# Projection chunks spread over the transform stages of a fused Hyena and pooling layer

## What is computed

```python
u = h * (1.0 + scale[:, None, :]) + shift[:, None, :]
proj = u @ w_in[layer] + b_in[layer]
hy_streams, hy_gate, pool_in, pool_gate = jnp.split(proj, splits, axis=-1)
k_freq = _hyena_filters_freq(...)
y_h = _hyena_branch(hy_streams, conv_w[layer], conv_b[layer], k_freq, hyena_bias[layer])
y_p = _pool_branch(pool_in, pool_w[layer], pool_scale[layer])
y = jnp.concatenate([y_h * silu(hy_gate), y_p * silu(pool_gate)], axis=-1)
out = gate[:, None, :] * (y @ w_out[layer] + b_out[layer])
h = _layer_norm(DEEPNORM_ALPHA * h + out, ln_g[layer], ln_b[layer])
```

## Time and profile before

| | us |
|---|---|
| median of 3 runs | 1505.89 |
| lowest, highest | 1505.31, 1510.5 |
| the profiled execution, its own time | 1512.34 |
| its span | 1510.6 |
| TensorE busy in the span | 1226.2 |
| VectorE, ScalarE, GpSimd busy | 837.5, 461.6, 427.1 |

### The profile page before, as it was taken

The page is one execution under the profiler, slowest core; times in us unless marked ns, Lnnn a source line. Parts: engine busy times, 40 slices in busy tenths (PEclk is TensorE's granted clock), DMA queues, the critical chain, the costliest instruction groups (busy, mean ns, idle before and its releaser), DMA issues. The chain is left out here.

```text
span 1510.6 us, 14907 instructions
## 1 busy us (share of the span) xinstructions
PE 1226.2 (81%) x5260; PEld 943.8 (62%) x5260; DVE 837.5 (55%) x784; ACT 461.6 (31%) x619; POOL 427.1 (28%) x236
## 2 busy tenths in 40 slices
PE   3788956489999999999999953784757855699996
PEld 1356734378888888888888732553545534488884
...
GB/s 316 76 258 318 308 348 407 325 134 56 56 112 79 87 168 36 62 83 56 8 49 56 28 249 341 235 275 191 353 333 248 338 207 325 205 168 85 105 89 69
DMA packets 170488, 273.50 MB, mean 181 GB/s; under 512 B 24007, under 2 KB 70087, under 8 KB 167626
## 3 DMA queue, kind: packets, MB, share of 16 engines
...
## 5 line engine op out<-in xcount | busy, mean ns | idle before, releaser
L136 PE MATMUL prj_pp<-u_uhi,prj_whi 128*128 128x512 f32 x768 | 300.2, 391 | 0.2 <-POOL u_ulo L800 0.2
L138 PE MATMUL prj_pp<-u_uhi,prj_wlo 128*128 128x512 f32 x768 | 299.0, 389 | 0.0
L137 PE MATMUL prj_pp<-u_ulo,prj_whi 128*128 128x512 f32 x768 | 299.0, 389 | 0.0
L136 PEld LDWEIGHTS prj_pp<-u_uhi,prj_whi 128*128 128x128 f32 x768 | 144.2, 188 | 30.6 <-issue 0.6
L138 PEld LDWEIGHTS prj_pp<-u_uhi,prj_wlo 128*128 128x128 f32 x768 | 144.2, 188 | 30.4
L137 PEld LDWEIGHTS prj_pp<-u_ulo,prj_whi 128*128 128x128 f32 x768 | 144.2, 188 | 29.5
L808 POOL CAST prj_whi<-prj_ws 128x1024 fp32r<-128x1024 f32 x22 | 23.9, 1086 | 392.5 <-DMA prj_ws<-in_w_in 230.3
L899 ACT ACTIVATE prj_row<-prj_pp,prj_bcol 128x512 f32<-128x512 f32 x64 | 43.9, 688 | 291.1 <-PE prj_pp L138 253.7
L1001 DVE TENSOR_SCALAR prj_cv<-prj_row,prj_cw,prj_cb 128x2048 f32<-128x2048 f32 x12 | 16.2, 1347 | 191.6 <-PE prj_px L844 103.9
L1284 POOL TENSOR_TENSOR sp_y<-sp_by_re,sp_by_im 128x512 f32<-128x512 f32 x32 | 68.2, 2132 | 191.1 <-DVE sp_by_im L1355 191.1
L136 PE MATMUL sp_u<-sp_ahi,spec_fwd 128*128 128x512 f32 x128 | 57.2, 447 | 62.3 <-DVE sp_alo L1335 62.3
(11 more groups left out here) (186 smaller groups left out, 2476.6 us busy)
## 6 DMA issues: line engine op xcount, KB each, us to landing
kseq<-fs_xo SPq DMA_DIRECT2D x32, 512.0 KB, 4.1
fs_a<-kseq SPq DMA_DIRECT2D x32, 512.0 KB, 8.6
kfreq<-fs_out SPq DMA_DIRECT2D x32, 512.0 KB, 9.2
sp_a<-xseq SPq DMA_DIRECT2D x32, 512.0 KB, 5.9
...
bseq<-sp_out SPq DMA_DIRECT2D x32, 512.0 KB, 3.5
prj_ws<-in_w_in SPq DMA_DIRECT2D x24, 512.0 KB, 6.4
...
```

The lines of the kernel that those rows point to most:

```text
L136: nc.tensor.matmul(out, w[0], m[0], start=start, stop=False, skip_group_check=True)
L137: nc.tensor.matmul(out, w[0], m[1], start=False, stop=False, skip_group_check=True)
L138: return nc.tensor.matmul(out, w[1], m[0], start=False, stop=stop, skip_group_check=True)
```

## The change

The projection is no longer a stage. `uhi` and `ulo` (both 64 KB in each partition) are made once and stay in SBUF from the second filter stage to the end of the pooling, and the 96 chunks are written into the other stages: 16 in `values_and_filters` (the old `filter_stage2` with the making of u and the tiles of v), 8 in `signal_stage1`, 16 in the first `spectrum_product`, 8 in `between_orders`, 16 in the second `spectrum_product`, and 32 in a stage `pooling` of their own, with the pooling sums. The class `Projection` holds the resident data, two PSUM banks `pp` and one buffer `ws` for raw weights; `Turned` and `Gated` hold the work that follows a chunk. The stages are named p1 to p6 in the tiles.

The rings are shorter: in `spectrum_product` one buffer each for `ahi`, `alo`, `u`, `y`, `by_im`, `yhi`, `ylo`, `b`, `out` and two for `a` and `kf`; in `between_orders` one `xhi`, one `xlo` and two of the rest, before four.

Also: x and `w_in` come already transposed or tiled as inputs (`t_xt`, `t_win`), so the 128 transposes of x go away; the filter's first step works on pairs of 64-row matmuls without GpSimd's copy `hs`; the forward first step of the signal too (6 half matmuls for 6 whole ones, a table of half the size); the table copies `w1f`, `kgen` to `i1` are made in `front`, those of `w1s` and `iw1` in p1; and the loads of `ya` (4 MB) and `gate_bias` move from sp1 into `last_inverse`.

The core of the diff:

```diff
+    def half_chunk(self, pe, q, half):
+        n, c, b, bank = q // 4, q % 4, q // 4 % 2, q % 2
+        if half == 0:
+            if c == 0:
+                pe.wait_ge(self.wlo_done[b], n // 2 + 1)
+            after(pe, self.bank_read[bank], q // 2)
+        cols = slice(c * CH, (c + 1) * CH)
+        for k in range(4 * half, 4 * half + 4):
+            mm = mm3(self.nc, self.pp[bank][:, :], (self.whi[b][:, k, :], self.wlo[b][:, k, :]),
+                     (self.uhi[:, k, cols], self.ulo[:, k, cols]), k == 0, k == KT - 1)
+        if half == 1:
+            mm.then_inc(self.prj_done[bank], 1)
...
+def values_and_filters(nc, t, tabs, pj, scale1, shift, kseq, kfreq, vx):
...
+        chunk_at = {2 + 2 * q if q < 4 else 9 + 3 * (q - 4) // 2: q for q in range(16)}
+        form_at = {step: (2 * step, 2 * step + 1) for step in range(8)}
+        conv_at = {step + 2: q // 4 for step, q in chunk_at.items() if q % 4 == 3}
+        turn_at = {step + 1 + part: (i, part) for step, i in conv_at.items() for part in range(4)}
...
+            for step in range(S):
+                if 0 <= step - 1 < N:
+                    unit(step - 1)
+                q = due(chunk_at, step)
+                if q is not None:
...
+                    pj.chunk(pe, q)
+                if due(turn_at, step) is not None:
+                    tn.turn(pe, *turn_at[step])
```

In `spectrum_product` (TensorE, VectorE; `conv_at` is every fourth step from 5):

```diff
-            staggered(NU, (fwd, 0), (inv, 3))
+            for step in range(S):
+                if step < NU:
+                    fwd(step)
+                if step < 16:
+                    pj.chunk(pe, q0 + step)
+                if 0 <= step - 1 < NU:
+                    inv(step - 1)
+                if tn and step in turn_at:
...
+                            tn.turn(pe, i, part)
...
-            staggered(NU, (alow, 0), (ylow, 3), (multiply, 1), (real_to_y, 1))
+            for step in range(S):
+                if step < NU:
+                    alow(step)
...
+                if tn and step in conv_at:
+                    tn.conv(dve, conv_at[step])
...
+                if 0 <= step - 1 < NU:
+                    ylow(step - 1)
+                if step < NU:
+                    multiply(step)
```

In `between_orders` (TensorE; SyncE's loads):

```diff
-            staggered(GS, (inv, 0), (fwd, 4))
+            for step in range(S):
+                if step < GS:
+                    inv(step)
+                c = due(chunk_at, step)
+                if c is not None:
+                    pj.half_chunk(pe, q0 + c, 0)
+                if 0 <= step - 3 < GS:
+                    fwd(step - 3)
+                if c is not None:
+                    pj.half_chunk(pe, q0 + c, 1)
...
+                    after(sp, xlo_done, n - 1)
+                    sp.dma_start(x[r][:, :, :], group_rows(bseq, n)).then_inc(x_in[r], 16)
+                    after(sp, inv_done[r], n // 2)
+                    sp.dma_start(f32(itab[r][:, :, :, :]), tabs["iw1"][n, :, :, :, :]).then_inc(itab_in[r], 16)
+                    after(sp, z_done[r], n // 2)
+                    sp.dma_start(x1[r][:, :], vx[:, n, DH:2 * DH]).then_inc(x1_in[r], 16)
```

More of the change, by code:

```diff
@@ L507, in gen @@
             def gen(n):
[L508 to L516 removed]
+                r, g, o = n % 2, n // 2, n % 2
@@ new lines, in _ @@
+            for step in range(S):
+                if step in form_at:
+                    for m in form_at[step]:
+                        form_u(m)
+                if step < N:
+                    low(step)
+                if 0 <= step - 2 < N:
+                    evac(step - 2)
+                if due(conv_at, step) is not None:
+                    if conv_at[step] == 0:
+                        for b in range(4):
+                            dve.wait_ge(ulo_done[b], 4)
+                    tn.conv(dve, conv_at[step])
+                if step in form_at:
+                    low_u(form_at[step][0])
@@ L646, in evac @@
             def evac(n):
[L647 to L670 removed]
+                dve.wait_ge(mm_done[n % 2], n // 2 + 1)
@@ new lines, in evac @@
+                after(dve, stored[n % 3], 16 * (n // 3))
+                nc.vector.tensor_copy(xo[n % 3][:, 1, :], ps[n % 2][:, 1, :]).then_inc(out1[n % 2], 1)
+            for step in range(S):
+                if step < GS:
+                    low(step)
+                if 0 <= step - 2 < GS:
+                    evac(step - 2)
+                c = due(chunk_at, step - 2)
+                if c is not None and c == 3:
+                    gt.conv(dve, 0)
+                if c is not None and c >= 4:
+                    gt.gate(dve, 0, c - 4)
@@ L1495, in last_inverse @@
[L1495 removed]
+def last_inverse(nc, t, tabs, bseq, rows, g2, ya, gate_bias, whl):
     with Scope(nc, "fin") as s:
```

1744 lines of the change are left out of this document (918 added, 826 removed).

## The result

The changed kernel takes 1446.23 us (median of 4 runs, 1443.97 to 1448.84). The kernel before, run beside it, takes 1505.83 (1505.31 to 1510.5). The ratio is 0.9598, with a 95% interval of 0.957 to 0.9626. It is faster, as forecast, but by 60 us where 126 were forecast, and 1446 lies above the range of 1338 to 1440.

What follows compares the result with a forecast made beforehand. The prediction saw the projection bound by matmuls while other stages left TensorE idle, so chunks would fill that idle time. Ten stage lengths summed to 1384.6 us, giving a median of 1380, range 1338 to 1440.

Steps and rivals of the forecast that it cites:

- TensorE's step is fwd 12 slots (2.72), chunk (5.45), inv (1.36): 9.53 us.: p3, also used for p5: TensorE's time per step, forward matmuls, one chunk and inverse pairs, 9.53 us.
- Both are under 9.53, so TensorE bounds.: p3: `alo` ready at 7.9 us and the single `y` loop of 8.6 both fit within TensorE's step.
- Path (b): p3: the loop closed by the single `y`, through products, `y`, `yhi`, `ylo` and four hand-offs, 8.6 us.
- A convolution ahead of `ylo` moves alo to about 10.8, 1.3 late, three times (4); the weight split on GpSimd costs about 2.: p3: small additions to the stage, 4 us for convolutions and about 2 for the weight split.
- if a release in SyncE's queue holds loads that are due sooner: One of two stated conditions under which the forecast falls; no size given.
- Until the last piece of x has landed SyncE has issued ... 18.0 MB: 47 us at 382 GB/s.: Front of p1: costed as transfers, 54 us with start and constants, chunk 3 ending at 64.
- a step without chunk takes 3.8 ... 7.5: p4: two step lengths, 3.8 us without a chunk and 7.5 with one; 8 x 3.8 + 7 x 7.5 = 83.
- term for late loads of x (8): p4: x loaded only a step ahead, 1 us a pair taken, 8 us in all; bounds 0 and 27.
- 8 chunks and 16 units of 3 slots: 43.6 + 10.9: p2: TensorE's work, to which start 7, convolution 1 and end 6 were added for 69 us.
- 1386 and 1380.: Whole kernel: profiled run 1.7 us above the stage sum of 1384.6, and the median, with 0.43% taken off.
- the loop of 8.6 us: p3: products, `y`, `yhi`, `ylo` and hand-offs around the single `y` buffer take 8.6 us a step.
- short rings and late loads: Rival: p4 waits the full landing (+19), kfreq's `out` buffers and p1's transfers (+15); 1415 to 1445 us, chance 0.10.

Runs made afterwards that it cites:

- k11: Changed kernel with p3 and p5 convolutions over a 32nd of their row and only 3 of each chunk's 24 matmuls there; 1415.1 us, one run.
- k4: Changed kernel with 21 of the 24 matmuls of each chunk in p3 and p5 left out; 1431.74 us, one run.
- k1: Changed kernel with p3's stores of vx issued one step earlier, ahead of the load of kfreq; 1433.36 us.
- k2: Changed kernel with the six small vectors loaded as one table by one DMA; 1443.18 us.
- k5: k2 plus p1's first weight tile loaded earlier and split behind GpSimd's low parts of steps 0 and 1; 1436.2 us.
- k6: k5 plus ScalarE instead of VectorE scaling and shifting every second piece of x in p1; 1439.22 us.
- k7: Changed kernel with the two halves of each chunk in p4 placed in two successive steps; 1436.31 us.

## Why the prediction was wrong, point by point

The direction held, and the mechanism in the main: the chunks fill TensorE's idle time, and TensorE bounds most steps of p3 and p5. The size failed in the steps below, and the two largest are these: the stores of vx in p3, which the sum left out (16.4 us), and the front of p1, costed as a transfer where VectorE's cycle bounds it (10.7 us).

**"TensorE's step is fwd 12 slots (2.72), chunk (5.45), inv (1.36): 9.53 us."** A mis-sized term: it measured 10.02. One slot for a pair of 64-row matmuls is right inside the group, but the changes of shape cost some 0.4 us a step. In all, 15 x 0.5 = 7.5 us in p3 and as much in p5. In p5 the last forward step nevertheless ended 162.2 after the start (161 forecast), since convolutions, weight splits and slow first matmuls took less than their terms, and the drain took 20 instead of 16. The same switch makes p4's pair dearer (12.1 against 11.3) and p2's (7.27 against 6.8, 4 us in all).

**"Both are under 9.53, so TensorE bounds."** Right for most steps, by a smaller margin than stated. Path (b) left out that GpSimd splits a weight tile in every fourth step, which makes `ylo` 3.4 us and the loop 10.5 to 11.0 (k11), and that a convolution makes it 12.7 (k4). TensorE's chunk covered nearly all of this: p5's waits for `alo` are 0.56 us, twice.

**"A convolution ahead of `ylo` moves alo to about 10.8, 1.3 late, three times (4); the weight split on GpSimd costs about 2."** Over-forecast: in k1, where nothing else disturbs, the waits for `alo` are 0.73, 0.33 and 0.33. With the transposes, k1's fifteen steps take 156.7 us, 10.45 on the mean, and its last forward step ends at 166.8 where the forecast had 168. The two errors cancel.

**What the forecast of p3 left out: the stores of vx.** The stores of the turned tiles were in no term but as the word "store" in the drain, neither their place behind the load of kfreq in SyncE's queue nor the ring of two buffers that makes ScalarE wait for them. They cost 16.4 us, shown by k1: the largest single item. It is near the kind that the text itself names ("if a release in SyncE's queue holds loads that are due sooner"), but here stores were held, and through them ScalarE. The other 4 us of p3 are its drain: 27 in k1, 23 forecast.

**"Until the last piece of x has landed SyncE has issued ... 18.0 MB: 47 us at 382 GB/s."** The wrong bound: the front of p1 was costed as a transfer. It is a cycle on VectorE (6.5 us a step), and before that two waits of equal length, one hidden behind the other: the small vectors in SyncE's queue and the weight split in GpSimd's. Against the changed kernel's 200.5, k2 took away one alone (1.2 us less, not clear of p1's own spread of 3.4), k5 both (4.6), k6 shortened the cycle too (7.8, chunk 3 at 66.3). The forecast had priced transfers and TensorE but gave no sum for VectorE here. Chunk 3 came 10.7 us late, the end of the stage 5 more; the parts of the forecast add up to 184.5, for which it wrote 186. The lengthening by GpSimd, which it had read in the earlier trace rows for `ylo` and used in p3, applied here too (3.04 against 1.22).
The forecast weighed 382 GB/s against the some 358 that the Trainium skill ("DMA: Bandwidth & Descriptors", Specifications) gives as a limit. k6's front moved 404 GB/s for 20 us, so the measurement stands above that figure once more.

**p4: "a step without chunk takes 3.8 ... 7.5"** measured 4.02 and 8.08, and 9.7 in four of the seven pairs: what was left out is that a gap of 1.57 us, which the forecast's own 3.8 contains, can be followed by matmuls at 0.43 us. That costs 1.6 us each time, and k7 shows it by taking the gap away. The part from the last inverse step on took 20 where 16.5 were forecast. The term for late loads of x (8) was too large: TensorE's long waits are for `xlo`, and ScalarE waited for x for 2 us outside the start. p4 of k7 is 112.7, though under the forecast's 116.

**p2: "8 chunks and 16 units of 3 slots: 43.6 + 10.9".** Besides the switches, one wait of 4.01 us (TensorE for `xo`, VectorE's copy behind the convolution) where 1 was allowed. No experiment was made on it, so the cause of p2's 8.3 us is read from its rows only.

**"1386 and 1380."** The sum missed by 58 us, 1380 by 66. The forecast took 0.43% off because the profiled execution of the kernel before lay that far above its median; that of the changed kernel (1444.37) lies 1.9 us below its median. The place of one execution in its spread does not carry over to another kernel.

**Right:** front's copies are hidden (DMA share 0.81, 71.3 us); filter_stage1 without the decay wait (its DMA share is 0.97 at 326 GB/s from 110 to 150; that transfers bound it no run tests); pooling; fin's wait for `ya` (10.2 us where 7 were forecast); the loop of 8.6 us in a step where GpSimd splits no weights (k11: 8.3 to 8.8). One reading was off without a term resting on it: filter_stage1 left TensorE idle for 17% of its time before, not a quarter.

The rival "short rings and late loads" (1415 to 1445, chance 0.10) came nearest: the result is 1.2 us above its range. That is partly luck, since its items were others: a ring did bind, in p3's `st`, not in p4 or kfreq. The lesson for the range: the sum had ten terms, and in nearly each of those that failed, what lay beside the busy times (waits, changes of shape, drains) was put too low, so the errors mostly had the same sign and did not cancel.
